# Merging input norm, projection and HGRN of a hybrid encoder layer into one block with interleaved TensorE work

## What is computed

```python
h = rmsnorm(x, norm_mix_pre)
z = h @ w_in                       # 1024 x 2976 columns
cq, ckv, kr, hq, hff, hfb, hi, hg = split(z)    # 256, 128, 32, then 5 x 512
a = rmsnorm(mla(cq, ckv, kr, ...))
# HGRN: 4 heads, forward and backward direction, chunks
f = lb + (1 - lb) * sigmoid(f_pre); kk = 1 - f; q = silu(hq)
o = scores @ v + (q * decay) @ state            # in each chunk
r = rmsnorm(o_forward + o_backward) * silu(hg)
x = x + rmsnorm(concat(a, r) @ w_o)
x = x + rmsnorm(square(relu(rmsnorm(x) @ w_up)) @ w_down)
x = x + rmsnorm((p @ w_ple) * sigmoid(x @ w_ple_gate))
```

## Time and profile before

| | |
|---|---|
| median of 3 runs | 1712.37 us (1711.17 to 1715.15) |
| profiled execution, its own time | 1711.46 us |
| its span, first to last instruction | 1709.6 us |
| PE busy | 1540.0 us (90%) |
| PE weight loads busy | 1249.0 us (73%) |
| DVE, ACT, POOL busy | 663.0, 470.5, 503.6 us |
| mean granted TensorE clock | 0.953 |

### The profile page before, as it was taken

The page is one execution under the profiler, slowest core; times in us unless marked ns, Lnnn a source line. Parts: engine busy times, 40 slices in busy tenths (PEclk is TensorE's granted clock), DMA queues, the critical chain, the costliest instruction groups (busy, mean ns, idle before and its releaser), DMA issues.

```text
span 1709.6 us, 20112 instructions
## 1 busy us (share of the span) xinstructions
PE 1540.0 (90%) x7208; PEld 1249.0 (73%) x7208; DVE 663.0 (39%) x997; ACT 470.5 (28%) x882; POOL 503.6 (29%) x439
## 2 busy tenths in 40 slices
PE   2999999666668999899889999999999999998996
PEld 2778888556664577687678888888888888876775
DVE  5001111478756565544452041414141414145453
ACT  5012221222221444544441121212121212134342
POOL 1222222455510010144542222222222222234563
PEclk8999999898877999999999999999999999999998
DMA  3111111000013000152231111111111111122223
GB/s 131 45 49 45 47 49 31 0 1 0 0 30 63 7 1 0 29 200 79 86 99 38 50 50 49 44 49 50 50 46 47 50 49 50 46 67 90 75 93 130
DMA packets 51063, 90.50 MB, mean 53 GB/s; under 512 B 11440, under 2 KB 13488, under 8 KB 50992
## 3 DMA queue, kind: packets, MB, share of 16 engines
q1 hardware_dynamic: 50560, 89.02, 17.1%
q10 hardware_dynamic: 432, 0.53, 0.1%
HBM read 83.24 MB, written 4.19 MB: 51 GB/s over the span
## 4 chain that ended last, share of the span: by engine, by line
PE 50%; DVE 3%; issue 2%; POOL 2%; ACT 1%; DMA 0%; DVEq 0%; ACTq 0%
PE ps L111 16%; PE ps L113 16%; PE ps L112 16%; PE ps L1641 1%; POOL wy_low L1327 1%; DVE hid_low L1437 1%; POOL y_stat L1332 1%; ACT junk_y L1223 0%; DVE hg_vg L1371 0%; DVE x_res L1495 0%; DVE total L1492 0%; DVE h_tile L1413 0%; ACT junk_y L1168 0%; DMA gain<-in_att_out_norm 0%; DVE a_low L1378 0%
## 5 line engine op out<-in xcount | busy, mean ns | idle before, releaser
L1327 POOL TENSOR_TENSOR wy_low<-w_raw,wy_high 128x512 fp32r<-128x512 f32 x216 | 293.9, 1362 | 632.0 <-ACT wy_high L1151 632.0
L1151 ACT ACTIVATE wy_high<-w_raw 128x512 fp32r<-128x512 f32 x216 | 136.2, 631 | 663.8 <-PE ps L113 659.2
L111 PE MATMUL ps<-wy_high,hid_high 128*128 128x512 f32 x512 | 202.5, 395 | 15.9 <-DVE hid_low L1437 10.0
L111 PE MATMUL ps<-a_high,wy_high 128*128 128x512 f32 x512 | 200.2, 391 | 1.7 <-DVE a_low L1378 1.7
L112 PE MATMUL ps<-wy_low,hid_high 128*128 128x512 f32 x512 | 201.0, 393 | 0.0
L113 PE MATMUL ps<-wy_high,hid_low 128*128 128x512 f32 x512 | 200.7, 392 | 0.0
L112 PE MATMUL ps<-a_low,wy_high 128*128 128x512 f32 x512 | 199.9, 390 | 0.0
L113 PE MATMUL ps<-a_high,wy_low 128*128 128x512 f32 x512 | 199.7, 390 | 0.0
L1462 DVE TENSOR_TENSOR total<-total,ps 128x512 f32<-128x512 f32 x112 | 76.1, 687 | 154.7 <-PE ps L113 154.7
L1421 DVE TENSOR_SCALAR relu<-ps 128x512 f32<-128x512 f32 x32 | 22.0, 686 | 284.0 <-PE ps L113 283.5
L111 PEld LDWEIGHTS ps<-wy_high,hid_high 128*128 128x128 f32 x512 | 97.2, 190 | 40.4 <-issue 20.6
(11 more groups left out here) (192 smaller groups left out, 2525.2 us busy)
## 6 DMA issues: line engine op xcount, KB each, us to landing
w_raw<-in_w_up SPq DMA_DIRECT2D x72, 256.0 KB, 2.7
w_raw<-in_w_down SPq DMA_DIRECT2D x72, 256.0 KB, 2.7
w_raw<-in_w_in SPq DMA_DIRECT2D x40, 256.0 KB, 2.6
w_raw<-in_w_o SPq DMA_DIRECT2D x32, 256.0 KB, 2.8
w_raw<-in_w_ple_gate SPq DMA_DIRECT2D x32, 256.0 KB, 2.7
x_tile<-in_x SPq DMA_DIRECT2D x8, 512.0 KB, 5.1
x_res<-in_x SPq DMA_DIRECT2D x8, 512.0 KB, 5.5
y<-x_res SPq DMA_DIRECT2D x8, 512.0 KB, 3.3
```

The costliest lines, as they stand in the source:

```text
L111: pe.matmul(out, stat_high, mov_high, start=start, stop=False)
L1151: act.activation(wy_high[:, n % PAIRS, :], w_raw[:, n % RING, :], ACT.Copy).then_inc(high_made, 1)
L1327: pool.tensor_tensor(wy_low[:, n % PAIRS, :], w_raw[:, n % RING, :], wy_high[:, n % PAIRS, :].bitcast(F32), ALU.subtract).then_inc(low_mad ...
```

## The change

The first three blocks become one. The program of every engine is written out without loops, over these tables:

- `units`: one unit of projection output each. Wide units, ("v", s) and ("hg", s), are the values and gates of one sequence: 8 chunks of 12 matmuls on 4 banks, one weight tile a chunk. The others are one head's q, f or b, one latent part or the rope columns for both sequences: 4 chunks of 12 matmuls on 2 banks, one weight tile every two chunks. Such a tile holds four blocks of 128 rows by 128 columns, read in pieces of 128 columns.
- `fill`, `slots`, `after`, `more`: which chunks stand behind which step of a head. Ahead of head 0 come v of sequence 0, q, f, b of head 0 and v of sequence 1 (28 chunks, 336 matmuls). The other 68 chunks (816 matmuls) stand inside the heads: 16 in each of heads 0, 1 and 3 and 20 in head 2; two of them (24 matmuls) behind the second sequence's product of each level, one behind the first key transposes and one behind the chunk products.
- The latent columns come in heads 0 to 2, the gate in head 3, q, f, b of a head in the head before it.

`hg_z` holds one head instead of four. A level's product has one bank for each sequence (4 and 5) instead of two, and so waits until DVE has read the level before out of it. The pairs of `w_high` and `w_low` are three instead of two; ACT and POOL make a tile two tiles ahead of its use. PE turns four token tiles, and then the other four between the first chunks; x is loaded into eight tiles without a wait. ACT evicts half of v (DVE the other half) and all of the latent; sigmoids of q, f, b are evicted through `sig`. In the MLP, from f = 1 on, a down product waits for the one half of the hidden tile that it reads.

```diff
-class Weights:
-    ...
-        with ExitStack() as c:
-            x_tile = sb(c, "x_tile", [P, TRIP, D])
-            ...
-            with nc.Block() as block:
-                ...
-        hg_z = sb(hg, "hg_z", [P, 3, HH, T])
-        with ExitStack() as c:
-            w = Weights(nc, c, "p2", w_raw, w_high, w_low, KD, [KD - 1])
-            ...
+        heads = [[("q", 0), ("f", 0), ("b", 0)] if j == 0 else [] for j in range(HH)]
+        units = [("v", 0)] + heads[0] + [("v", 1)]
+        fill = [[("q", 1), ("f", 1), ("b", 1), ("lat", 0)], [("q", 2), ("f", 2), ("b", 2), ("lat", 1)],
+                [("q", 3), ("f", 3), ("b", 3), ("lat", 2), ("rope", 0)], [("hg", 0), ("hg", 1)]]
+        for j in range(HH):
+            units += fill[j]
+        unit_at = {unit: u for u, unit in enumerate(units)}
+        banks_x = {("v", 0): [0, 1, 2, 3], ("q", 0): [4, 5], ("f", 0): [6, 7], ("b", 0): [0, 1], ("v", 1): [2, 3, 6, 7],
+                   ("hg", 0): [2, 3, 0, 1], ("hg", 1): [2, 3, 0, 1], ("rope", 0): [0, 1]}
+        for j in range(HH):
+            banks_x["lat", j] = [2, 3]
+            if j:
+                banks_x["q", j], banks_x["f", j], banks_x["b", j] = [0, 1], [2, 3], [0, 1]
+        wide = ("v", "hg")
+        tiles_x = [(unit, c) for unit in units for c in range(8 if unit[0] in wide else 2)]
+        tile_at = {tile: n for n, tile in enumerate(tiles_x)}
+        chunks = [(unit, c) for unit in units for c in range(8 if unit[0] in wide else 4)]
+        XTILES, XPAIRS, XAHEAD = len(tiles_x), 3, 2
+        SIGMOIDS = [unit for unit in units if unit[0] in ("q", "f", "b", "hg")]
+        ...
+        slots = [("kq", 0), ("kq", 1)] + [("lv", l, g) for l in range(LEVELS) for g in range(2)]
+        slots += [("kt", 0), ("kt", 1), ("kv", 0), ("kv", 1), ("o", 0), ("o", 1)]
+        after = {("kt", 0): 1, ("kv", 1): 1}
+        after.update({slot: 2 for slot in slots if slot[0] == "lv" and slot[2] == 1})
+        more = {("kq", 1): 1, ("kt", 1): 1, ("o", 0): 1, ("o", 1): 1}
+        first_chunk = chunks.index((fill[0][0], 0))
+        placed_x, taken = {}, first_chunk
+        for j in range(HH):
+            for slot in slots:
+                n = after.get(slot, 0) + (more.get(slot, 0) if j == 2 else 0)
+                placed_x[j, slot] = chunks[taken:taken + n]
+                taken += n
+        assert taken == len(chunks)
+        ...
+        z = at("hg_z", [P, 3, T], F32, total_at_byte + 16384)
+        ...
+                @block.gpsimd
+                    ...
+                    for j in range(HH):
+                        for slot in slots:
+                            if slot[0] == "lv" and slot[2] == 1:
+                                decay_keys(j, slot[1])
+                            ...
+                                if unit[0] in wide or k % 2 == 0:
+                                    low(tile_at[unit, k if unit[0] in wide else k // 2] + XAHEAD)
+                @block.scalar
+                    ...
+                    late = [units[unit_at["q", 1] - 1]]
+                    for j in range(HH):
+                        for slot in slots:
+                            if slot[0] == "kq" and j:
+                                pick_keys(j, 0, slot[1])
+                            elif slot[0] == "lv" and slot[1] < LEVELS - 1:
+                                pick_keys(j, slot[1] + 1, slot[2])
+                            elif slot[0] == "kt":
+                            ...
+                                evict(unit)
+                            late = []
+                            for unit, k in placed_x[j, slot]:
+                                if unit[0] in wide or k % 2 == 0:
+                                    high(tile_at[unit, k if unit[0] in wide else k // 2] + XAHEAD)
+                                if k == (7 if unit[0] in wide else 3):
+                                    late.append(unit)
+                @block.vector
+                    ...
+                    for j in range(HH):
+                        for slot in slots:
+                            if slot == ("kq", 0) and j:
+                                queries_of(j, 0)
+                                queries_of(j, 1)
+                            if slot[0] == "kq":
+                                own_scores(j, slot[1])
+                            elif slot[0] == "lv":
+                                level(j, slot[1], slot[2])
+                            elif slot[0] == "kv":
+                                states(j, slot[1])
+                            ...
+                @block.tensor
+                    ...
+                    def chunk(unit, k):
+                        kind, j = unit
+                        banks = banks_x[unit]
+                        if kind in wide or k % 2 == 0:
+                            pe.wait_ge(w_low_made, tile_at[unit, k if kind in wide else k // 2] + 1)
+                        if kind in wide:
+                            n = tile_at[unit, k]
+                            wh, wl = wx_high[n % XPAIRS][:, :], wx_low[n % XPAIRS][:, :]
+                            for i in range(4):
+                                if k == 0:
+                                    free(unit, i)
+                                    if kind == "v":
+                                        pe.wait_ge(split, 2 * (4 * j + i) + 2)
+                                rows = slice((4 * j + i) * P, (4 * j + i + 1) * P)
+                                made = three_passes(pe, ps[:, banks[i], :], h_high[:, k, rows], h_low[:, k, rows], wh, wl,
+                                                    k == 0, k == KD - 1)
+                                if i == 3 or k == 7:
+                                    made.then_inc(done, 1)
+                            return
+                        n, width = tile_at[unit, k // 2], columns(unit)[1]
+                        for kd in (2 * k, 2 * k + 1):
+                            cols = slice(kd % 4 * P, kd % 4 * P + width)
+                            for i in range(2):
+                                if kd == 0:
+                                    free(unit, i)
+                                    if j == 0 and kind == "q":
+                                        pe.wait_ge(split, 2 * (4 * i + 3) + 2)
+                                half = slice(i * BANK, (i + 1) * BANK)
+                                made = three_passes(pe, ps[0:width, banks[i], :], wx_high[n % XPAIRS][:, cols],
+                    ...
+                    def level(j, l, g):
+                        pe.wait_ge(k_picked, j * (2 * LEVELS) + 2 * l + g + 1)
+                        if l:
+                            pe.wait_ge(q_decayed, j * (2 * LEVELS) + 2 * (l - 1) + g + 1)
+                        else:
+                            pe.wait_ge(q_made, j * 2 + g + 1)
+                        pe.wait_ge(level_read, j * (2 * L1) + 2 * l + g + 1)
+                        for ch in range(CHUNKS):
+                            last = pe.matmul(ps[:, 4 + g, ch * P:(ch + 1) * P], k_pick[:, g, l % 2, ch * P:(ch + 1) * P],
+                                             halves(qq, g, l, True, ch, 1), start=True, stop=True)
+                        last.then_inc(level_full, 1)
+                    ...
+                    pe.wait_ge(consts, 3)
+                    for t in range(4):
+                        turn(t)
+                    for n, (unit, k) in enumerate(chunks[:first_chunk]):
+                        chunk(unit, k)
+                        if n < 4:
+                            turn(4 + n)
+                    step = {"kq": own, "lv": level, "kt": keys_turned, "kv": products, "o": outputs}
+                    for j in range(HH):
+                        for slot in slots:
+                            step[slot[0]](j, *slot[1:])
+                            for unit, k in placed_x[j, slot]:
+                                chunk(unit, k)
...
-                        elif kind in ("dn8", "dn4") and i == 0:
-                            pe.wait_ge(hid_made, 8 * f + (4 + k if f == 0 else 2 * k + 1) + 1)
+                        elif kind in ("dn8", "dn4") and f == 0 and i == 0:
+                            pe.wait_ge(hid_made, 4 + k + 1)
+                        elif kind == "dn8" and i % 4 == 0 or kind == "dn4" and i == 0:
+                            pe.wait_ge(hid_made, 8 * f + 2 * k + (i // 4 if kind == "dn8" else h) + 1)
```

More of the change, by code:

```diff
@@ new lines, in trunk_kernel @@
+        SIGMOIDS = [unit for unit in units if unit[0] in ("q", "f", "b", "hg")]
+        ended, count = {}, 0
+        for unit, c in chunks:
+            if unit[0] in wide:
+                for i in range(4 if c == 7 else 1):
+                    count += 1
+                    ended["bank", unit, i] = count
+                ended["tile", tile_at[unit, c]] = count
+            elif c in (1, 3):
+                for i in range(2 if c == 3 else 1):
+                    count += 1
+                    ended["bank", unit, i] = count
```

(50 more changed lines are left out.)

911 lines of the change are left out of this document (448 added, 463 removed).

## The result

| | before | after |
|---|---|---|
| median, us (range) | 1712.23 (1711.17 to 1715.15) | 1594.76 (1591.88 to 1595.42) |
| ratio after/before | | 0.9308, 95% interval 0.9292 to 0.9325 |
| span of the profiled execution | 1709.6 | 1590.1 |
| first projection matmul | 42.58 | 19.09 |
| attention's first load | 506.51 | 390.02 |

The kernel is 6.9% faster. The mechanism is the one forecast, and 10 us more came of it. Nearly all of the gain lies ahead of attention's first load: 116.5 of the 119.5 us between the two profiled executions.

What follows compares the result with a forecast made beforehand. PE bounds the projection, a chain round the engines HGRN. Start 19.3, turns 4.0, projection 270.7, HGRN's PE work 101.6, stalls 7.0 and last copy 0.9 make 403.5 instead of 506.51; with 5.0 from the MLP, 1605 us, range 1594 to 1628.

Steps and rivals of the forecast that it cites:

- start: Before the projection: first projection matmul at about 19.3 us instead of 42.58, between 16 and 26 possible.
- levels, with 4.0 of stalls at turns: HGRN levels in four heads: PE's own products, 57.4 us, plus 1 us of stall at each head's turn, 4.0.
- other own work of four heads: HGRN on PE besides levels: own scores 2.1, transposes 1.53, chunk products 2.84, outputs 4.57 us a head; 44.2 in all.
- gate units: Head 3: the gate's four banks must be read before the second gate unit may start, about 3 us, once.
- DVE not the bound: HGRN levels: DVE stays under 7.69 us a level; the rival, DVE the bound and kernel slower, 1765 us, chance 0.01.
- weights on time: Projection weight loads: late weights cost nothing unless a load takes over 15 us; this rival had no chance of its own.
- The projection matmuls cost what they cost before: 1152 x 0.235: Projection on PE: 270.7 us, 79 of them ahead of head 0 and 191.7 in the heads.
- Levels 7 x 2.05: HGRN in each head: PE's products of seven levels at 2.05 us each, 14.4 us a head.
- The bound for stalls: Stalls at head turns and gate: 7.0 us taken; bounds 0, and today's 19.2 for `k_sum` with 7.7 for states.
- Together 5.0: MLP up to down turns: finer waits win 5.0 of PE's 10.0 us waiting for hid_low; bounds 0 and 6.
- bare head ends: Rival at head ends: waits for `k_sum` and states stay whole, 27 us instead of 4, giving 1628; chance 0.12.
- the chain that adds itself: Rival in HGRN levels: chain starts too late, a level takes 9.3 us, 45 us more, giving 1650; chance 0.04.

Runs made afterwards that it cites:

- a_head3: Changed kernel with head 3's 16 chunks taken out of its levels and key and state products, 8 put behind each of its two output products: 1608.61 us.
- a_12each: Changed kernel with a level's 24 projection matmuls split, 12 behind each sequence's product: 1594.17 us.
- a_twice: Changed kernel with each level product issued twice, 448 more matmuls of 128 columns: 1645.47 us.
- b_pad: Kernel before with only 96 unused bytes added at the upper end of SBUF, which moves h_high and h_low: 1701.46 us, ratio 0.994.
- a_h32: Changed kernel with h_high and h_low 32 bytes higher: 1599.15 us.
- better: Changed kernel with other banks for the first gate unit and, in heads 0 and 1, a level 6 chunk moved behind the second own scores: 1590.62 us.
- a_h64: Changed kernel with h_high and h_low 64 bytes higher: 1598.36 us.
- after_again: Changed kernel run once more, unedited, beside the second run of `better` on the same chip: 1593.44 us, ratio 0.9307.

## Why the prediction was right in its mechanism and short in its sum

The block, term by term, in us, in the profiled execution of after (heads by head 1, whose start and end the timelines show):

| term of the sum | forecast | measured | from |
|---|---|---|---|
| start | 19.3 | 19.1 | first projection matmul |
| ahead of head 0, with four turns | 79.0 + 4.0 | 83.6 | 19.09 to 102.67 |
| 68 chunks in the heads | 191.7 | 185.0 | 68 x 12 x 0.2267 |
| levels, with 4.0 of stalls at turns | 57.4 + 4.0 | 54.8 | 4 x (51.79 - 14 x 2.72) |
| other own work of four heads | 44.2 | 42.8 | 4 x (67.93 - 16 x 2.72 - 13.7) |
| gate units | 3.0 | 2.6 | wait for `hg_vg` |
| end | 0.9 | 2.1 | what is left |
| attention's first load | 403.5 | 390.0 | |

(51.79 is head 1's stretch from 172.98, its level 0, to 217.53 + 7.24, the end of its level 6; 67.93 its whole, 170.81 to 238.74.)

- **Right**: the start within 0.2 us; the clock at 1.00 in the heads; waits for `k_pick` and `k_sum` gone; head ends covered, DVE not the bound; weights on time (no wait for a load). `a_head3`, `a_12each` and `a_twice` bear out the mechanism behind it: chain under cover, PE's queue the sum of what stands in it.
- **The step that failed most: "The projection matmuls cost what they cost before: 1152 x 0.235".** They took 0.2267 in the steady state, which makes this term 9.6 us too large. The cause is not in the schedule but in an address, shown from both sides: `b_pad` gained 7.5 us in the projection and 6.9 at attention's first load, `a_h32` lost 7.5 there (1152 x 0.0066 to 0.0076 = 7.6 to 8.8). Ahead of head 0 the gain is hidden in the table by turns, slow first matmuls and 1.6 us of waits for `wx_low`, together 7.4 (83.6 - 336 x 0.2267) where I had 4.0. The full change holds the `edge` and the new addresses, though the excerpt of it above doesn't show them; I had passed over them as unused memory.
- **"Levels 7 x 2.05" was mis-sized**: 2.05 was the busy length of a group of pipelined records, which counts the last one's tail. What PE's queue pays is start to start: 2.59, 1.83 and 1.70. With the turn stalls, of which `better` could win only 0.3 to 0.6 a head, that is 6.6 us. The bound for stalls reached down to 0, but these two errors were in terms that I had given no range. The range had a slip of its own: its lower end, 1594, adds up all lower bounds, but all upper ones (start 6.7, stalls 9, MLP 5) give 1626 and not 1617.
- **"Together 5.0" of the MLP wait** was too much: the wait at each turn went, but 0.35 us of its 0.56 came back at the next one, the ReLU reads, which I had put 0.6 us inside their time; and the last turn won nothing, one wait of 2.2 for two of 2.0 together. About 1 us stayed.
- The rivals: bare head ends cost 1.2 to 1.3 us each and not 5.8; the chain that adds itself would have shown in `a_head3` as more than 25 us, which cost 13.8. The 3.0 us less behind attention's first load are the MLP's 0.8 and the spread of the rest; in the repetition of after only 0.4 of them are left (1202.7).

## What to carry to other kernels

When a change makes one engine's queue the bound, price each piece by the distance between starts in that queue, not by busy lengths, and look at matmuls of the same shape apart if they read their operands in another pattern. Read a diff for addresses too: a padding that does no work can be worth as much as a step of the schedule, and the cheapest test is that line alone in the old kernel. A wait made finer gives back only as much as the next wait behind it allows; a split of covers (12 and 12, or 24) is worth nothing while the chain has slack.

## What the runs showed of the hardware

- **An operand's start address sets the matmul rate.** With `h_high` and `h_low` at multiples of 128 bytes, 512-column fp32r matmuls start 0.2267 us apart. At 64 above such a multiple (`a_h64`): 0.2333 where `h` is stationary, the moving operand left where it was, and 0.229 to 0.2333 where it is moving. At 96 above (before): 0.2333 (moving) and 0.2343 (stationary), and at 32 above (`a_h32`) 0.2333. Other operands and types were not tried.
- **The moving operand's pattern does too.** A level's eight matmuls of 128 f32 columns take 2.59 us where the pattern alternates between two places after each element (level 0 of head 1; 3.05 in head 0, where the chunk moved by `better` brought it to 2.52), 1.83 after two, 1.70 after four and more (levels 2 and up). `a_twice` shows that it is the matmuls that are slow; that the pattern is the reason is argued, as no run changed the pattern alone. The Trainium skill has a rule of this kind ("SBUF — State Buffer", Door 1: The DMA port swizzle): the memory has lines of 16 bytes, four f32, and wants at least two hits in a line to keep its bandwidth. By that rule, level 0 alone is slow and level 1 at the edge; the trace agrees, with 52% and 8% more than level 2.
- **The gain in the projection is rate, not clock**: from 46 to 305 us the granted clock was 1.00 in before and in `b_pad`.
- **A short stretch of low clock has a price of its own**: `after_again` had a granted clock of 0.98 in head 3 where after had 1.00, with the same waits, and took 1.4 us longer for it. From 353.9 to 357.3 us it had the low level (0.51), and nowhere else in that head.
